# A decoder layer on one core: two norms' squares summed by GpSimd, the last norm applied by rows and stored in quarters

## The chip, the cores and the metric

The kernel runs on one core of a Trainium2 chip. The metric is the device time of one execution in microseconds (us), and the comparison is by the median of several executions. A core has TensorE (matmuls; PE in the profile, its weight loads PEld), VectorE (DVE), ScalarE (ACT), GpSimd (POOL) and SyncE (SP), each with its own instruction stream. They wait for each other by semaphores only, and 16 transfer engines move data on their behalf.

## The reference, cut to what matters

One step of a decoder layer on 256 prompt tokens and 8 sample tokens, 264 columns in all, with 2048 channels. The mixer in front of these lines (gated DeltaNet and a short convolution) is not touched.

```python
def rmsnorm(x, g):
    r = xf * lax.rsqrt(jnp.mean(xf * xf, axis=-1, keepdims=True) + EPS)
    return r * g
...
    h = h + mixed @ w_o
    hn = rmsnorm(h, ffn_norm)
    h = h + (jax.nn.silu(hn @ w_ffn_gate) * (hn @ w_ffn_up)) @ w_ffn_down
    hn = rmsnorm(h, ple_norm)
    h = h + jax.nn.sigmoid(hn @ w_ple_gate) * (p_i @ w_ple_proj)
...
    y_prompt = rmsnorm(hp, final_norm)
    y_sample = rmsnorm(hs, final_norm)
```

## The kernel before, in words

The activations lie transposed in SBUF: `h` has 16 tiles of 128 channels by 264 tokens. Every weight matrix is streamed once from memory, in *pieces* of 4 x 128 rows by 256 columns (512 KB; 3 or 2 x 128 rows in the down projections, 2 in the ple projection). SyncE loads a piece into one of four `raw` buffers (L447), ScalarE rounds it into `whi` (L951), VectorE subtracts to get `wlo` (L1238), and TensorE multiplies each 128-row slice and each of two 128-column tiles three times (L675): xhi by whi, xlo by whi, xhi by wlo, 24 matmuls a piece. Splits run three pieces ahead (`AHEAD`). Four pieces over all 2048 rows make a *pair* of output tiles in two PSUM banks, and pairs alternate between banks 0, 1 and banks 2, 3.

The order is written out by hand: a list of phases, each with its pairs, and every engine walks this list with its own code for each piece (`extra(ph, it, j)`, j the piece in the phase) and each pair (`evac`). At the end of the list stand `wo`, then `ffn0r`, `ffn0s`, `down0` and `ffn1r`, `ffn1s`, `down1` (the two halves of the ffn), `pproj` (the ple projection) and the ple gate, eight pairs in three phases, `pgate_first`, `pgate` and `pgate_last`. `wo`, `down0`, `down1` and `pgate` are loops with two pairs in the body.

A norm works so: ScalarE squares each of the 16 tiles of `h` into `sqh` (L961), TensorE multiplies each by a matrix of ones and adds them up in bank 4 (`norm_sums`), VectorE makes the mean and its reciprocal (L1270, L1272), ScalarE the root, and every pair is multiplied by `rstd` at its eviction (L1487). So the weights can be multiplied by the unnormed, gain-scaled `h` first. For the ffn and the ple norm four squares and four sums follow each of the phase's first four pieces. For the final norm two squares and two sums follow each of the first seven pieces of `pgate_last`, and the last two come behind the last pair. Then VectorE multiplies the 16 tiles by gain and `rstd` (L1646), TensorE turns them in blocks of 128 by 128 (L926), ScalarE copies them out of PSUM (L1224), and SyncE stores 128 rows at a time (L460) and then the 8 sample rows (L462).

A gate pair is evicted in three steps: VectorE multiplies by `rstd` (L1487), ScalarE takes the sigmoid (L1122), VectorE multiplies by the projection `pp` and adds to `h` (L1500, L1505).

Of the kernel before, what the change touches and what calls it, by code (L numbers as in the profile page):

```python
# [35 lines left out]
ds = bass.ds  # L36
# [54 lines left out]
def trunk(nc, I, O):  # L91
# [120 lines left out]
    sqh = at("sqh", [P, DTL, N], F32, regO)  # L212
# [12 lines left out]
    with ctx:  # L225
# [91 lines left out]
        def layer_pairs(gx):  # L317
# [12 lines left out]
            Phase("wo", 4, [mk(wo, lambda it, n=n: (2 * it + n) * COLS, X, "addh", (lambda it, n=n: 2 * it + n), xr="mix") for n in range(2)]),  # L330
# [5 lines left out]
        for half in range(2):  # L336
            for part, lo_, n_ in (("r", 0, FP - NB), ("s", FP - NB, NB)):
# [86 lines left out]
        NORM = {"first": 0, "ffn0r": 1, "pgate_first": 2}  # L424
        PREV = lambda ph: phases[phases.index(ph) - 1]

        def vcol(i):
            return vec[:, ds(i, 1)]
# [5 lines left out]
        def _(sp):  # L434
# [235 lines left out]
        def _(pe):  # L670
# [6 lines left out]
            def norm_sums(n, tiles=range(DTL)):  # L677
# [5 lines left out]
                if tiles[-1] == DTL - 1:  # L683
                    m.then_inc(sum_ready, 1)
# [991 lines left out]
```

## Time and profile before

| | |
|---|---|
| three runs | 2762.25, 2772.05, 2767.54 us; median 2767.54 us |
| the profiled execution | 2767.79 us; its span 2766.3 us, mean granted TensorE clock 0.982 |
| busy, share of the span | TensorE 96%, VectorE 60%, ScalarE 48%, GpSimd 16% |
| chain that ended last | TensorE 58%, transfers 2%, VectorE, GpSimd and ScalarE 1% each |
| moved | 505.25 MB, mean 183 GB/s |

The chain is followed back from the last instruction, at each step to what released it. Where it names TensorE's matmul line, nothing held TensorE. Times in the rows are us from the start of the span, unless a column says ns. A row `[0.87 <-ACT sqh L961]` means that the engine stood idle for 0.87 us before it, until that line of that engine had finished. An fp32 matmul with the ones stands as two instructions in the trace, so `x8` there are four sums.

### The profile page before, as it was taken

How to read it: one execution, taken by the hardware profiler on the slowest of the kernel's cores; microseconds unless marked ns; L12 is line 12 of the kernel's file. 1: busy time of each engine (PE TensorE's matmuls, PEld its weight loads, DVE VectorE, ACT ScalarE, POOL GpSimd, SP SyncE). 2: the span in 40 equal slices, each digit the busy share in tenths (PEclk: the TensorE clock that was granted, in tenths of full speed). 3: DMA queues.
4: the chain of work that ended last, by engine and by line, in shares of the span. 5: the costliest groups of instructions: out<-in, count | busy, mean ns of one | idle time of the engine just before them, and what ended most of it. 6: DMA issues, size and time to landing. Idle time of an engine off the chain costs nothing.

```text
span 2766.3 us, 54613 instructions
## 1 busy us (share of the span) xinstructions
PE 2641.9 (96%) x21133; PEld 2597.2 (94%) x21133; DVE 1653.7 (60%) x2851; ACT 1325.2 (48%) x2010; POOL 453.6 (16%) x845
## 2 busy tenths in 40 slices
PE   6999999999999999999999999999999999999997
PEld 4999999999999999999999999999999999999997
DVE  4757576666757475633354555456676656776664
ACT  5526454453535353443443344344665545655553
POOL 1425160515243341000000000000110000100000
PEclk9999999999999999999999999999999999999998
DMA  5545464545545555767655555746997567985542
GB/s 167 163 136 159 133 173 116 173 136 154 143 141 141 154 144 146 207 190 214 201 171 183 167 167 166 252 141 194 304 319 248 181 195 233 320 275 185 172 159 82
DMA packets 441663, 505.25 MB, mean 183 GB/s; under 512 B 19521, under 2 KB 421690, under 8 KB 438658
## 3 DMA queue, kind: packets, MB, share of 16 engines
q1 hardware_dynamic: 415264, 415.42, 49.2%
q0 software_dynamic: 25664, 87.47, 10.1%
q8 instruction: 107, 1.75, 0.3%
q14 instruction: 50, 0.41, 0.0%
q10 hardware_dynamic: 578, 0.19, 0.0%
HBM read 477.10 MB, written 26.49 MB: 182 GB/s over the span
## 4 chain that ended last, share of the span: by engine, by line
PE 58%; DMA 2%; DVE 1%; POOL 1%; ACT 1%; issue 1%; DVEq 0%; ACTq 0%; SPq 0%; POOLq 0%
PE bank L675 57%; DMA raw<-in_w_o 1%; POOL sol L546 1%; POOL prod L543 0%; ACT xhi L965 0%; DMA raw<-in_w_ffn_down 0%; DVE xlo L1266 0%; DVE wlo L1238 0%; ACT whi L951 0%; DMA blk<-blk_scratch 0%; DVE h L1646 0%; PE bank L926 0%; DMA raw<-in_w_ple_gate 0%; DMA DT<-sol_scratch 0%; DMA sol_scratch<-sol 0%
## 5 line engine op out<-in xcount | busy, mean ns | idle before, releaser
L675 PE MATMUL bank<-xhi,whi 128*128 128x264 f32 x5520 | 1602.7, 290 | 36.9 <-DVE wlo L1238 16.5
L675 PE MATMUL bank<-xlo,whi 128*128 128x264 f32 x5520 | 1573.9, 285 | 0.0
L675 PE MATMUL bank<-xhi,wlo 128*128 128x264 f32 x5520 | 1571.3, 285 | 0.0
L1238 DVE TENSOR_TENSOR wlo<-raw,whi 128x1024 fp32r<-128x1024 f32 x828 | 1009.9, 1230 | 824.5 <-ACT whi L951 823.0
L951 ACT ACTIVATE whi<-raw 128x1024 fp32r<-128x1024 f32 x828 | 870.9, 1057 | 854.2 <-PE bank L675 763.1
L675 PEld LDWEIGHTS bank<-xhi,whi 128*128 128x128 f32 x5520 | 1047.0, 190 | 44.3 <-issue 37.1
L675 PEld LDWEIGHTS bank<-xlo,whi 128*128 128x128 f32 x5520 | 1047.5, 190 | 2.6 <-issue 1.9
L675 PEld LDWEIGHTS bank<-xhi,wlo 128*128 128x128 f32 x5520 | 1044.6, 189 | 0.0
L675 PE MATMUL bank<-ahi,whi 128*128 128x264 f32 x704 | 200.7, 285 | 2.0 <-DVE wlo L1238 2.0
L675 PE MATMUL bank<-ahi,wlo 128*128 128x264 f32 x704 | 200.8, 285 | 0.0
L675 PE MATMUL bank<-alo,whi 128*128 128x264 f32 x704 | 200.4, 285 | 0.0
L675 PEld LDWEIGHTS bank<-ahi,whi 128*128 128x128 f32 x704 | 133.1, 189 | 2.2 <-DVE wlo L1238 2.2
L675 PEld LDWEIGHTS bank<-ahi,wlo 128*128 128x128 f32 x704 | 133.3, 189 | 0.0
L675 PEld LDWEIGHTS bank<-alo,whi 128*128 128x128 f32 x704 | 133.0, 189 | 0.0
L546 POOL TENSOR_TENSOR sol<-sol,prod 128x60 f32<-128x60 f32 (+24 forms) x248 | 123.8, 499 | 19.5
L648 POOL DMA_DIRECT2D out_gdn_s<-sS x16 | 18.7, 1171 | 607.6 <-DVE sS L1603 607.6
L543 POOL TENSOR_TENSOR prod<-blk,sol 128x60 f32<-128x60 f32 (+24 forms) x248 | 114.7, 462 | 19.5
L1383 DVE SCALAR_TENSOR_TENSOR cacc<-cin,vec,cacc 128x288 f32<-128x288 f32 x224 | 108.4, 525 | 4.0
L1157 ACT ACTIVATE sS<-sS,bc 128x128 f32<-128x128 f32 x256 | 81.2, 392 | 0.0
L1603 DVE SCALAR_TENSOR_TENSOR sS<-sD,kqs,sS 128x128 f32<-128x128 f32 x256 | 72.6, 346 | 0.0
L520 POOL DMA_DIRECT2D st_qkv<-in_state_qkv_conv x32 | 16.8, 528 | 292.0 <-PE bank L675 292.0
L675 PEld LDWEIGHTS bank<-kqs,chunkS 128*128 128x128 f32 x512 | 62.8, 191 | 0.0
(280 smaller groups left out, 1846.2 us busy)
## 6 DMA issues: line engine op xcount, KB each, us to landing
raw<-in_w_in SPq DMA_DIRECT2D x356, 512.0 KB, 3.9
raw<-in_w_ffn_gate SPq DMA_DIRECT2D x88, 512.0 KB, 5.5
raw<-in_w_ffn_up SPq DMA_DIRECT2D x88, 512.0 KB, 4.8
raw<-in_w_ffn_down SPq DMA_DIRECT2D x96, 384.0 KB, 2.9
raw<-in_w_gdn_out SPq DMA_DIRECT2D x64, 512.0 KB, 3.3
chunkS<-in_state_gdn POOLq DMA_DIRECT2D x16, 1024.0 KB, 7.4
raw<-in_w_sconv_out SPq DMA_DIRECT2D x32, 512.0 KB, 3.4
raw<-in_w_o SPq DMA_DIRECT2D x32, 512.0 KB, 3.3
```

What stands on the lines that cost most here:

```text
L520: pool.dma_start(st_qkv[:, i % 2, :, :], stq[:, ds(STATE_COL[i](grp), COLS)].rearrange("r (t p) -> r t p", p=P)).then_inc(st_in[i % 2], 16)
L543: mine.inc(pool.tensor_tensor(prod[:, 0:m, 0:n], blk[:, j, j + 1:SB].unsqueeze(1).to_broadcast([P, m, n]), sol[:, 0:m, j:j + 1].to_broadca ...
L546: mine.inc(pool.tensor_tensor(sol[:, 0:m, j + 1:SB], sol[:, 0:m, j + 1:SB], prod[:, 0:m, 0:n], ALU.add))
L648: pool.dma_start(O["gdn_s"][0, 2 * b2 + s, 16 * c:16 * c + 16, :, :].rearrange("h k v -> k h v"), sS[:, s, :, :]).then_inc(n_stored[s], 16)
L675: return pe.matmul(out, lhsT, rhs, start=start, stop=stop)
L951: act.activation(whi[:, at_ % SPLIT, :, :], raw[:, at_ % RAW, :, :], ACT.Copy).then_inc(hi_ready, 1)
L1157: m = act.activation(sS[:, s, i, :], sS[:, s, i, :], ACT.Copy, scale=bc[:, ds(it * 2 + (s + 1), 1), 16 * c + i:16 * c + i + 1].rearrange(" ...
L1238: dve.tensor_tensor(wlo[:, at_ % SPLIT, :, :], raw[:, at_ % RAW, :, :], f32(whi[:, at_ % SPLIT, :, :]), ALU.subtract).then_inc(lo_ready, 1)
L1383: m = dve.scalar_tensor_tensor(out=cacc[:, t, :], in0=x, scalar=w, in1=cacc[:, t, :], op0=ALU.mult, op1=ALU.add)
L1603: m = dve.scalar_tensor_tensor(out=sS[:, s, i, :], in0=sD[:, s, i, :], scalar=kqs[:, 8 * c + i // 2, ds(it * 2 + s, 1), 0], in1=sS[:, s, i ...
```

## The change

- `wo`, `down0`, `down1` and the ple gate become one written-out phase each, with eight pairs.
- In `wo` and `down1` ScalarE squares each finished pair of `h` in one instruction of 528 elements (`acc_square`), the first into `acc`, the others into `et`, behind the second split of the next pair; the eighth comes in the next phase's first piece. GpSimd adds them into `acc` (`squares_in`). TensorE sums over the partitions with two matmuls behind the third piece (`acc_sums`).
- In the gate phase TensorE turns a finished pair of `h` into banks 5, 6 and 7 (two prompt blocks and the 8 sample rows), behind piece 4i+6 (`turn_out`). ScalarE squares these with an accumulator into a column of `ssum` (`out_squares`), VectorE multiplies them by the final gain into `yrow` (`out_gains`). The gain stands along the row, so GpSimd loads a copy of it for each of the 128 partitions.
- Behind the last pair VectorE adds the eight columns of `ssum`, and mean, reciprocal and root work on three columns (`rs`). Then ScalarE scales block 0, VectorE block 1 and GpSimd the sample rows by `rs`. Blocks 0 and 1 are done and stored in quarters of 512 channels.

```diff
-            Phase("wo", 4, [mk(wo, lambda it, n=n: (2 * it + n) * COLS, X, "addh", (lambda it, n=n: 2 * it + n), xr="mix") for n in range(2)]),
+            Phase("wo", 1, [mk(wo, lambda it, n=n: n * COLS, X, "addh", const(n), xr="mix") for n in range(NPB)]),
...
-        phases.append(Phase("pgate_first", 1, [mk(wpg, lambda it, n=n: n * COLS, X, "pg", const(n), xr="ple") for n in range(2)]))
-        phases.append(Phase("pgate", NPB // 2 - 2, [mk(wpg, lambda it, n=n: (2 * it + n) * COLS, X, "pg", (lambda it, n=n: 2 * it + n), xr="ple") for n in (2, 3)]))
-        phases.append(Phase("pgate_last", 1, [mk(wpg, lambda it, n=n: n * COLS, X, "pg", const(n), xr="ple") for n in (NPB - 2, NPB - 1)]))
+        phases.append(Phase("pgate", 1, [mk(wpg, lambda it, n=n: n * COLS, X, "pg", const(n), xr="ple") for n in range(NPB)]))
...
+        def turned_at(ph, j, lag):
+            i = (j - lag) // 4
+            return i if ph.name == "pgate" and j >= lag and (j - lag) % 4 == 0 and i < NPB - 1 else None
...
-            for b in range(BLK):
-                sp.wait_ge(y_copied, DTL // 4 * (b + 1))
-                sp.dma_start(yo[0, b * P:(b + 1) * P, :], yrow[:, b, :]).then_inc(out_stored, 16)
-            sp.wait_ge(y_copied, DTL // 4 * (BLK + 1))
+            for q in range(4):
+                c = slice(512 * q, 512 * q + 512)
+                for b in range(BLK):
+                    sp.wait_ge(y_out[b], q + 1)
+                    sp.dma_start(yo[0, b * P:(b + 1) * P, c], yrow[:, b, c]).then_inc(out_stored, 16)
+            sp.wait_ge(y_out[BLK], 1)
             sp.dma_start(O["y_sample"][:, 0, :], yrow[0:NB, BLK, :]).then_inc(out_stored, 16)
...
+            def squares_in(n):
...
+                for i in range(1, NPB):
+                    pool.wait_ge(acc_sq, NPB * n + i + 1)
+                    pool.wait_ge(acc_done, (NPB - 1) * n + i - 1) if n or i > 1 else None
+                    pool.tensor_tensor(acc[:, :, :], acc[:, :, :], et[:, 2 * (i % 2):2 * (i % 2) + 2, :], ALU.add).then_inc(acc_done, 1)
...
+            squares_in(0)
...
+            pool.memset(ssum[:, :, :], 1.0).then_inc(ssum_set, 1)
+            squares_in(1)
+            pool.dma_start(gain[:, :], I["final_norm"].partition_broadcast(P)).then_inc(gain_in, 16)
+            pool.wait_ge(rstd_ready, 4)
+            pool.wait_ge(y_gained, NPB)
+            pool.tensor_tensor(yrow[0:NB, BLK, :], yrow[0:NB, BLK, :], rs[0:NB, BLK:BLK + 1].to_broadcast([NB, D]), ALU.mult).then_inc(y_out[BLK], 1)
...
+            def acc_sums(n):
+                pe.wait_ge(acc_done, (NPB - 1) * n)
+                mm(bank[4][:, 0:N], ones[:, :], acc[:, 0, :], True, False)
+                mm(bank[4][:, 0:N], ones[:, :], acc[:, 1, :], False, True).then_inc(sum_ready, 1)
+            def turn_out(i):
+                freed(pe, by["pgate"], 0, i)
+                if i > 0:
+                    pe.wait_ge(y_gained, i)
+                for b in range(BLK + 1):
+                    r = P if b < BLK else NB
+                    for t in range(2):
+                        c = P * t
+                        m = pe.transpose(bank[5 + b][0:r, c:c + P], h[:, 2 * i + t, b * P:b * P + r], ident[:, :])
+                m.then_inc(y_turned, 1)
...
-                elif ph.name in NORM and j < 4:
-                    norm_sums(NORM[ph.name], range(4 * j, 4 * j + 4))
-                elif ph.name == "pgate_last" and j < 7:
-                    norm_sums(3, range(2 * j, 2 * j + 2))
+                elif ph.name == "first" and j < 4:
+                    norm_sums(range(4 * j, 4 * j + 4))
+                elif ph.name in ("ffn0r", "pgate") and j == 2:
+                    acc_sums(NORM[ph.name])
+                elif turned_at(ph, j, 6) is not None:
+                    turn_out(turned_at(ph, j, 6))
...
-            norm_sums(3, range(DTL - 2, DTL))
-            n = 0
-            for b in range(BLK + 1):
-                r = P if b < BLK else NB
-                for k4 in range(DTL // 4):
-                    pe.wait_ge(y_ready, 4 * k4 + 4)
-                    if n >= 4:
-                        pe.wait_ge(y_copied, n - 3)
-                    for k in range(4):
-                        m = pe.transpose(bank[n % 4][0:r, k * P:(k + 1) * P], h[:, 4 * k4 + k, b * P:b * P + r], ident[:, :])
-                    m.then_inc(y_turned, 1)
-                    n += 1
+            turn_out(NPB - 1)
...
+            def acc_square(ph, i):
...
+                n = NORM["ffn0r" if ph.name == "wo" else "pgate"] - 1
+                freed(act, ph, 0, i)
+                if i > 2:
+                    act.wait_ge(acc_done, (NPB - 1) * n + i - 2)
+                dst = acc[:, :, :] if i == 0 else et[:, 2 * (i % 2):2 * (i % 2) + 2, :]
+                act.activation(dst, h[:, 2 * i:2 * i + 2, :], ACT.Square).then_inc(acc_sq, 1)
+            def out_squares(i):
+                act.wait_ge(y_turned, i + 1)
+                if i == 0:
+                    act.wait_ge(ssum_set, 1)
+                c = slice(COLS * (i % 2), COLS * (i % 2) + COLS)
+                for b in range(BLK + 1):
+                    r = P if b < BLK else NB
+                    act.activation(junk[0:r, b, c], bank[5 + b][0:r, 0:COLS], ACT.Square, accum_out=ssum[0:r, b, i:i + 1]).then_inc(y_squared, 1)
...
+                elif q.kind == "addh":
+                    if ph.name in SUMMED and qi < NPB - 1:
+                        acc_square(ph, qi)
...
-                    if j == 0:
-                        freed_all(act, by["pgate"])
-                    elif j == 6:
-                        freed(act, ph, it, 0)
-                    squares(h, sqh, range(2 * j, 2 * j + 2))
+                if turned_at(ph, j, 7) is not None:
+                    out_squares(turned_at(ph, j, 7))
+                elif ph.name in ("ffn0r", "pproj") and j == 0:
+                    acc_square(by["wo" if ph.name == "ffn0r" else "down1"], NPB - 1)
...
-                        if q.kind in ("qkv", "sh") and qi + 1 < len(ph.pairs):
+                        if q.kind in ("qkv", "sh", "addh") and qi + 1 < len(ph.pairs):
                             late = qi
...
-            freed_all(act, by["pgate_last"])
-            squares(h, sqh, range(DTL - 2, DTL))
+            act.activation(junk[:, 0, 0:1], eps[:, :], ACT.Sqrt)
+            out_squares(NPB - 1)
             act.wait_ge(mean_ready, 4)
-            act.activation(rstd[:, :], rstd[:, :], ACT.Sqrt).then_inc(rstd_ready, 1)
-            n = 0
-            for b in range(BLK + 1):
-                r = P if b < BLK else NB
-                for k4 in range(DTL // 4):
-                    act.wait_ge(y_turned, n + 1)
-                    act.activation(yrow[0:r, b, k4 * 512:(k4 + 1) * 512], bank[n % 4][0:r, :], ACT.Copy).then_inc(y_copied, 1)
-                    n += 1
+            act.activation(rs[:, :], rs[:, :], ACT.Sqrt).then_inc(rstd_ready, 1)
+            act.wait_ge(rstd_ready, 4)
+            act.wait_ge(y_gained, NPB)
+            for q in range(4):
+                c = slice(512 * q, 512 * q + 512)
+                act.activation(yrow[:, 0, c], yrow[:, 0, c], ACT.Copy, scale=rs[:, 0:1]).then_inc(y_out[0], 1)
...
+            def out_gains(i):
+                if i == 0:
+                    dve.wait_ge(gain_in, 16)
+                for b in range(BLK + 1):
+                    r = P if b < BLK else NB
+                    dve.wait_ge(y_squared, (BLK + 1) * i + b + 1)
+                    m = dve.tensor_tensor(yrow[0:r, b, COLS * i:COLS * i + COLS], bank[5 + b][0:r, 0:COLS], gain[0:r, COLS * i:COLS * i + COLS], ALU.mult)
+                m.then_inc(y_gained, 1)
...
+                elif turned_at(ph, j, 7) is not None:
+                    out_gains(turned_at(ph, j, 7))
...
             walk(dve, work, (mine,), dve_per)
-            norm_mean(3)
-            for kt in range(DTL):
-                dve.scalar_tensor_tensor(out=h[:, kt, :], in0=h[:, kt, :], scalar=vec[:, 352 + kt:353 + kt], in1=rstd[:, :],
-                                         op0=ALU.mult, op1=ALU.mult).then_inc(y_ready, 1)
+            out_gains(NPB - 1)
+            for n in (4, 2, 1):
+                mine.inc(dve.tensor_tensor(ssum[:, :, 0:n], ssum[:, :, 0:n], ssum[:, :, n:2 * n], ALU.add))
+                mine.settle(dve)
+            mine.inc(dve.tensor_scalar(rs[:, :], ssum[:, :, 0], 1.0 / D, EPS, ALU.mult, ALU.add))
+            mine.settle(dve)
+            dve.reciprocal(rs[:, :], rs[:, :]).then_inc(mean_ready, 1)
+            dve.wait_ge(rstd_ready, 4)
+            dve.wait_ge(y_gained, NPB)
+            for q in range(4):
+                c = slice(512 * q, 512 * q + 512)
+                dve.tensor_scalar(yrow[:, 1, c], yrow[:, 1, c], rs[:, 1:2], None, ALU.mult).then_inc(y_out[1], 1)
```

How the instructions stand, at the places that the prediction speaks of. `L` is the line in the kernel of that list.

TensorE in `ffn0r`, before: the end of the first piece, its four sums, and the start of the second piece; three more such blocks follow.

```order
L675 MATMUL bank<-xhi,whi 128x264
L675 MATMUL bank<-xlo,whi 128x264
L675 MATMUL bank<-xhi,wlo 128x264
L675 MATMUL bank<-sqh,ones 128x264 x4
L675 MATMUL bank<-xhi,whi 128x264
L675 MATMUL bank<-xlo,whi 128x264
L675 MATMUL bank<-xhi,wlo 128x264
```

And now: the end of the third piece, and the only block of sums.

```order
L699 MATMUL bank<-xhi,whi 128x264
L699 MATMUL bank<-xlo,whi 128x264
L699 MATMUL bank<-xhi,wlo 128x264
L699 MATMUL bank<-acc,ones 128x264 x2
L699 MATMUL bank<-xhi,whi 128x264
L699 MATMUL bank<-xlo,whi 128x264
L699 MATMUL bank<-xhi,wlo 128x264
```

Sixteen sums in four blocks became two in one, two pieces later. ScalarE now, around the end of `wo` and the start of `ffn0r` (before it had no square in `wo`, and after the 16 scaled tiles four blocks of `sqh<-h 128x264 x4`, each behind a split):

```order
L998 ACTIVATE et<-h 128x528
L983 ACTIVATE whi<-raw 128x1024 x4
L998 ACTIVATE et<-h 128x528
L983 ACTIVATE whi<-raw 128x1024 x2
L1012 ACTIVATE xhi<-h,vec 128x264 x16
L983 ACTIVATE whi<-raw 128x1024
L998 ACTIVATE et<-h 128x528
L983 ACTIVATE whi<-raw 128x1024 x3
L1188 ACTIVATE rstd<-rstd 128x264
```

The squares moved ahead, between the splits of `wo`, and the last of them stands where the first four stood. TensorE in the gate phase now, between two pieces:

```order
L699 MATMUL bank<-xlo,whi 128x264
L699 MATMUL bank<-xhi,wlo 128x264
L724 MATMUL bank<-ident,h 128x128 x4
L724 MATMUL bank<-ident,h 8x128 x2
L699 MATMUL bank<-xhi,whi 128x264
L699 MATMUL bank<-xlo,whi 128x264
```

Six transposes stand where `pgate_last` had two sums. VectorE's last rows now, where it had 16 multiplies of `h`:

```order
L1563 TENSOR_TENSOR h<-h,et 128x264 x2
L1330 TENSOR_TENSOR yrow<-bank,gain 128x256 x2
L1330 TENSOR_TENSOR yrow<-bank,gain 8x256
L1706 TENSOR_TENSOR ssum<-ssum 128x3x4
L1706 TENSOR_TENSOR ssum<-ssum 128x3x2
L1706 TENSOR_TENSOR ssum<-ssum 128x3
L1708 TENSOR_SCALAR rs<-ssum 128x3
L1710 RECIPROCAL rs<-rs 128x3
L1715 TENSOR_SCALAR yrow<-yrow,rs 128x512 x4
```

Gain, sum of the columns, mean and reciprocal are followed by four quarters of block 1. GpSimd's last rows now (the loads of `prow` were its last before):

```order
L684 DMA prow<-in_p_sample 8x256
L685 MEMSET ssum 128x24
L667 TENSOR_TENSOR acc<-acc,et 128x528 x7
L687 DMA gain<-in_final_norm 128x2048
L690 TENSOR_TENSOR yrow<-yrow,rs 8x2048
```

Its queue goes on behind them with the adds of `down1`, the gain and the sample rows.

## Rows read from the trace of the kernel before

**Rows 1.** The chain that ended last: start us, us, what
```profile
1107.26 316.53 PE bank L675 x2644
...
1833.03 0.42 ACT sqh L961
1833.49 264.69 PE bank L675 x2156
...
2621.67 4.30 DMA raw<-in_w_ple_gate
```

**Rows 2.** Timeline of TensorE, norms' first pieces: start us, us, engine, line
```profile
1833.49 2.05 PE L675 MATMUL bank<-sqh,ones 128*128 128x264 f32 x8 [0.87 <-ACT sqh L961]
...
1847.68 1.94 PE L675 MATMUL bank<-sqh,ones 128*128 128x264 f32 x8
...
2635.42 2.05 PE L675 MATMUL bank<-sqh,ones 128*128 128x264 f32 x8 [0.70 <-ACT sqh L961]
```

**Rows 3.** Timeline of TensorE, the last two gate pairs
```profile
2713.62 1.16 PE L675 MATMUL bank<-sqh,ones 128*128 128x264 f32 x4 [1.03 <-ACT sqh L961]
...
2736.55 1.05 PE L675 MATMUL bank<-sqh,ones 128*128 128x264 f32 x4
```

**Rows 4.** Groups by line and form, GpSimd: busy us, mean ns | idle us
```profile
L539 POOL COPY sol<-unit 128x256 f32<-128x256 f32 x8 | 4.1, 511 | 49.1 <-DMA blk<-blk_scratch 49.1
...
L546 POOL TENSOR_TENSOR sol<-sol,prod 128x70 f32<-128x70 f32 x8 | 2.5, 315 | 0.6
...
L546 POOL TENSOR_TENSOR sol<-sol,prod 128x50 f32<-128x50 f32 x8 | 2.2, 276 | 0.6
```

**Rows 5.** Timeline of ScalarE, before the ple projection
```profile
2611.66 1.06 ACT L951 ACTIVATE whi<-raw 128x1024 fp32r<-128x1024 f32 x1
```

**Rows 6.** Windows: us, busy of PE PEld DVE ACT POOL, PEclk, DMA share, GB/s
```profile
2614.00:2618.00 4.00, 4.00 (x24) 4.00 (x24) 1.22 (x1) 2.36 (x6) 0.00 (x0) 0.65 0.20 66
2622.00:2626.00 4.00, 3.95 (x33) 3.74 (x31) 3.44 (x3) 3.47 (x8) 0.00 (x0) 1.00 0.85 275
```

**Rows 7.** Timeline of TensorE, the end
```profile
2755.78 6.25 PE L926 MATMUL bank<-ident,h 128*128 128x128 f32 x36 [0.50 <-DVE h L1646]
```

**Rows 8.** Window at the end, columns as in rows 6
```profile
2750.00:2760.00 10.00, 7.56 (x32) 6.36 (x33) 5.73 (x15) 4.09 (x7) 0.00 (x0) 0.50 0.17 68
```

**Rows 9.** Timeline of VectorE, the end
```profile
2742.90 0.78 DVE L1505 TENSOR_TENSOR h<-h,et 128x264 f32<-128x264 f32 x2
...
2749.17 6.56 DVE L1646 SCALAR_TENSOR_TENSOR h<-h,vec,rstd 128x264 f32<-128x264 f32 x16 [0.49 <-ACT rstd L1218]
```

**Rows 10.** Groups by line and form, ScalarE
```profile
L994 ACT ACTIVATE Tt<-bank 128x128 f32<-128x128 f32 x32 | 8.1, 254 | 3.1 <-PE bank L675 3.1
...
L994 ACT ACTIVATION_READ_ACCUMULATOR Tt<-bank 128x1 f32 x32 | 6.0, 188 | 0.0
...
L1224 ACT ACTIVATE yrow<-bank 128x512 f32<-128x512 f32 x8 | 4.8, 598 | 7.0 <-PE bank L926 7.0
```

**Rows 11.** Groups by line and form, VectorE
```profile
L1339 DVE TENSOR_SCALAR Nn<-kTok,tokk 128x128 f32<-128x128 f32 x64 | 13.2, 280 | 0.0
...
L1405 DVE TENSOR_SCALAR prep<-prep 32x264 f32<-32x264 f32 x1 | 0.3, 345 | 0.0
```

**Rows 12.** Timeline of VectorE, start of ffn0r
```profile
1833.16 1.23 DVE L1238 TENSOR_TENSOR wlo<-raw,whi 128x1024 fp32r<-128x1024 f32 x1 [0.45 <-ACT whi L951]
```

**Rows 13.** Timelines of VectorE and GpSimd, 383 to 388 us
```profile
383.51 3.83 DVE L1238 TENSOR_TENSOR wlo<-raw,whi 128x1024 fp32r<-128x1024 f32 x3
...
386.35 1.18 POOL L543 TENSOR_TENSOR prod<-blk,sol 128x75 f32<-128x75 f32 x1
387.61 0.35 POOL L546 TENSOR_TENSOR sol<-sol,prod 128x75 f32<-128x75 f32 x1
```

**Rows 14.** Timeline of SyncE, the end
```profile
2762.85 0.31 SPq L462 DMA_DIRECT2D out_y_sample<-yrow  x1
```

**Rows 15.** Transfers in 40 slices of 2756 to 2767 us
```profile
GB/s 0 0 0 60 0 0 0 0 209 417 328 477 477 477 447 357 357 268 0 0 0 477 477 477 447 387 328 357 387 477 239 0 0 0 0 0 0 0 0 0
```

More of the change, by code:

```diff
@@ L211, in trunk @@
     assert 8 * HALF * N + 16 * N <= 4 * (HV + DTL) * N
-    sqh = at("sqh", [P, DTL, N], F32, regO)
+    acc = at("acc", [P, 2, N], F32, regS + 17408)
+    ssum = at("ssum", [P, BLK + 1, NPB], F32, regS + 17408 + 2112)
+    rs = at("rs", [P, BLK + 1], F32, regS + 17408 + 2112 + 128)
+    junk = at("junk", [P, BLK + 1, 2 * COLS], F32, regS + 17408 + 2112 + 256)
+    assert regS + 17408 + 2112 + 256 + 8 * COLS * (BLK + 1) <= end
+    gain = at("gain", [P, D], F32, regO)
     prow = at("prow", [P, BLK + 1, PD], F32, regS)
@@ L423, in trunk @@
                     "first": {8: ("exponents",), 9: ("lt",)}}
[L424 to L428, printed above, removed]
+        NORM = {"first": 0, "ffn0r": 1, "pgate": 2}
+        SUMMED = ("wo", "down1")
+        def turned_at(ph, j, lag):
+            i = (j - lag) // 4
+            return i if ph.name == "pgate" and j >= lag and (j - lag) % 4 == 0 and i < NPB - 1 else None
         block = ctx.enter_context(nc.Block())
@@ L675, in mm, with norm_sums @@
                 return pe.matmul(out, lhsT, rhs, start=start, stop=stop)
-            def norm_sums(n, tiles=range(DTL)):
+            def norm_sums(tiles):
                 for kt in tiles:
-                    pe.wait_ge(sq_ready, DTL * n + kt + 1)
-                    src = sqr if n == 0 else sqh
-                    m = mm(bank[4][:, 0:N], ones[:, :], src[:, kt, :], kt == 0, kt == DTL - 1)
+                    pe.wait_ge(sq_ready, kt + 1)
+                    m = mm(bank[4][:, 0:N], ones[:, :], sqr[:, kt, :], kt == 0, kt == DTL - 1)
                 if tiles[-1] == DTL - 1:
                     m.then_inc(sum_ready, 1)
+            def acc_sums(n):
[12 more added lines that the diff above has]
+                m.then_inc(y_turned, 1)
             def gdn(slot, gr):
@@ L957, in split_ahead @@
                 split(it * (ph.pieces // RAW * 16) + 16 * (at_ // RAW + 1), at_, it * ph.pieces + at_ + 1)
-            def squares(src, dst, tiles):
-                for kt in tiles:
-                    act.activation(dst[:, kt, :], src[:, kt, :], ACT.Square).then_inc(sq_ready, 1)
+            def acc_square(ph, i):
[13 more added lines that the diff above has]
+                    act.activation(junk[0:r, b, c], bank[5 + b][0:r, 0:COLS], ACT.Square, accum_out=ssum[0:r, b, i:i + 1]).then_inc(y_squared, 1)
             def scaled_hi(gain):
@@ L1127, in extra @@
                     gdn(step, gr)
-                if ph.name == "pgate_last" and j < 7:
-                    if j == 0:
-                        freed_all(act, by["pgate"])
-                    elif j == 6:
-                        freed(act, ph, it, 0)
-                    squares(h, sqh, range(2 * j, 2 * j + 2))
+                if turned_at(ph, j, 7) is not None:
+                    out_squares(turned_at(ph, j, 7))
+                elif ph.name in ("ffn0r", "pproj") and j == 0:
+                    acc_square(by["wo" if ph.name == "ffn0r" else "down1"], NPB - 1)
                 elif ph.name in NORM and j < 4:
-                    squares(*((hpro, sqr) if ph.name == "first" else (h, sqh)), range(4 * j, 4 * j + 4))
+                    if ph.name == "first":
+                        for kt in range(4 * j, 4 * j + 4):
+                            act.activation(sqr[:, kt, :], hpro[:, kt, :], ACT.Square).then_inc(sq_ready, 1)
                     if j == 3:
```

19 lines of the change are left out of this document (11 added, 8 removed).

## Prediction

> **What bounds the kernel now.** I read the chain that ended last first. Through the body it is TensorE at its own pace: 316.53 us for 2644 matmuls in the written-out groups (0.120 us each), 264.69 us for 2156 from 1833.49 on (0.123, with one norm's sums among them) [rows 1]. There only less work on TensorE, or a wait before it that goes, shortens the run. After the last gate matmul (2740.5) the chain goes through every engine in turn, and there each handover counts. So I price four places: the ffn norm, the ple norm, the eight gate pairs, the end.
>
> **The two norms whose squares go to GpSimd.** Before, each of the first four pieces (24 matmuls) is followed by 4 sums. From the first block of sums to the fourth is 14.19 us, 4.73 a period [rows 2]; in the last gate pairs, with 2 sums a piece, six periods take 22.93 us, 3.82 each [rows 3]. The difference gives 0.455 us a sum and leaves 2.91 us a piece. 14 of 16 sums go: 14 x 0.455 = 6.4 us. TensorE also stood 0.87 us (ffn) and 0.70 us (ple) for the first squares [rows 2]. With the sums behind the third piece that wait goes, if the running sum is there. ScalarE makes the last square where its first one stood, at 1833.03 [rows 1], so it is there at about 1833.7; the third piece ends about 1838.4 (1833.49 - 0.87 + two pieces). GpSimd has 4.7 us for one add. No row has an add of 128x528; one of 128x50 takes 276 ns and one of 128x70 315 ns [rows 4]: 1.95 ns an element, 0.18 + 1.03 = 1.2 us. Bounds: nothing, or an add held by a VectorE split before it starts (1.23 us), together 2.4 us, still under 4.7. I take no cost. The seven adds before it have a pair of pieces each, 11.6 us, and ScalarE's seven squares in a phase lie behind a split, of which three are always ahead of TensorE. Gain: 7.3 us (ffn) and 7.1 us (ple).
>
> **The gain row.** GpSimd issues a new 1 MB transfer behind its last add. ScalarE squares the last down pair behind the split that begins at 2611.66 [rows 5]; with 0.6 us for the square and 1.2 for the add that is about 2614.5. The transfer engines carry little then (share 0.20 in 2614 to 2618) but 0.85 in 2622 to 2626 [rows 6], and the chain waits 4.30 us for w_ple_gate at 2621.67 [rows 1]. Bounds: nothing, and all of it, 3.8 us at that stretch's 275 GB/s. Most should fit in the quiet part; I take 1.0 us lost.
>
> **The gate pairs.** Out go 14 sums, 6.4 us, and a wait of 1.03 us [rows 3]. In come 7 x 6 transposes. At the end of before 36 of them take 6.25 us [rows 7] at a granted clock of 0.50 [rows 8], 1.04 us for six; at the full clock that would be 0.52. So seven sets cost 3.6 to 7.3 us; among full-clock matmuls, with a handover each, I take 5.0. Squares and gain multiplies (under 2 us a pair on engines that have 11.6) are hidden: pair i is turned after piece 4i+6, three pieces behind its last matmul, when its h is written. Gain 2.4 us. Writing the loops out costs nothing: loop and written-out stretches run alike [rows 1].
>
> **The end**, in the clock of before. The last h is there at 2742.90 + 0.78 = 2743.7 [rows 9].
> - Handover 0.2, six transposes at the low clock 1.3 with the last one's length: 2745.2.
> - Three squares with accumulator. A 128-wide one is 254 ns, a 512-wide eviction 598, so 256 wide is about 0.37, and a read of the accumulator 188 [rows 10], partly overlapped: 0.45 each, 2746.6. The last gain multiply 0.4: 2747.0.
> - Five operations on 3 columns, each behind the one before, at 0.2: 2748.0. Root: 2748.4. In before the first scaled h came at 2749.17, and 16 of them took 6.56 us more [rows 9]; transposes and evictions followed those.
> - Scaling. ScalarE's first quarter is there at 2749.0, then one each 0.5 us. VectorE: tensor_scalar took 280 ns for 128 columns and 345 for 264 [rows 11], 0.48 ns a column, against 1.2 in the two-input split (1.23 us for 1024 [rows 12]). 512 columns: 0.46 us. GpSimd: 8 rows, but 2048 elements in each: 0.18 + 2048 x 1.95 ns = 4.2 us.
>
> Here is the one new wait that matters. While VectorE ran three splits back to back (383.51 to 387.34), GpSimd's 75-element multiply took 1.18 us, and its next instruction of that size 0.35; VectorE took 3.83 us for the three instead of 3 x 1.23 [rows 13]. The two take a port in turns, an instruction at a time. I take it that the fast tensor_scalar needs what the splits need (no row shows it). So GpSimd's multiply slips in behind VectorE's first quarter (2748.9) and holds the other three until 2753.1. SyncE issues in order, block 0 then block 1 of each quarter: the fourth store waits until 2753.6, four more stand behind it at 0.4 each, and y_sample goes out at 2755.6. Before, y_sample's issue to the end was 2766.3 - 2762.85 = 3.45 us [rows 14], which gives 2759.1; the five late quarters of 256 KB, at about 400 GB/s [rows 15] 0.65 us each, run from 2754.4 to 2757.7 and end with 1.8 us of completion at 2759.5. The later one counts: the end gains 6.8 us.
>
> The Trainium skill, "SBUF — State Buffer", Who interferes with whom, has it as a rule: VectorE in a 2-port mode, or with two SBUF inputs, and GpSimd take the shared port pair as an exclusive lock for a whole instruction. By it VectorE stands for all of GpSimd's multiply; the trace agrees for short ones (1.18 against 0.35 us), and no row has a long one. The Trainium skill, "GPSIMD Engine Reference", 3.1 Elementwise, gives 4497 ns for a tensor_tensor add of 2048 fp32 elements; with it the end would be 0.3 us later than in my sum.
>
> **Sum.** 7.3 + 7.1 - 1.0 + 2.4 + 6.8 = 22.6 us. The profiled execution took 2767.8 us (the median of the three runs is 2767.5), so 2745.2, say **2745 us**. Its own range: gate transposes -1.4 or +2.3; the gain row +1.0 or -2.8; GpSimd's price per element 1.3 ns at the least, as in its 256-element copy (511 ns) [rows 4], 1.3 us earlier, and 4.5 ns at the most, if 315 ns for 70 had no fixed part, 5 us later. As they seldom fall together: 2742.5 to 2748.5.
>
> **Rivals.**
> 1. *No hold at the end.* VectorE's quarters all pass before GpSimd. The stores then run from 2750.0 at 0.65 us each to 2755.2, the end is 2757.2: 9.1 us instead of 6.8; with the gain row free 2742. For it: the four multiplies stand back to back, and both engines leave from one semaphore. Against: GpSimd got in between splits each time [rows 13]. 0.20.
> 2. *Transfer and port take more.* The gain row costs 3.8 us, and the last multiply holds 2 us longer: 2748.5 to 2751. For it the share of 0.85 [rows 6], against it the issue at about 2614.5. 0.15.
> 3. *The sums were not TensorE's bound.* ScalarE and VectorE come late out of the 16 tiles they scale and split. With the sums gone TensorE could wait for the fourth split, and half of each norm's gain is lost: 2752. Against: that split ends at 1834.4 [rows 12] and the fourth piece begins about 1839.3. 0.08.
> 4. *Slower.* Four phases written out add some 2300 matmuls to the program. If the supply of instructions slowed TensorE there (wo, down and gates are some 440 us, 3640 matmuls), 0.127 instead of 0.121 us each would eat the 22.6 us, and from 0.1295 us on (31 us lost, 2776) the kernel is slower. Against: the written-out groups run at 0.120 [rows 1]. 0.02.
>
> **How the numbers follow.** Main case 0.52, rival 1 0.20, rival 2 0.15, rival 3 0.08, rival 4 0.02, better than all 0.03. The range 2740.5 to 2751 leaves out rivals 3 and 4 and the better case, under 2 in 10. Within 0.3% (8.3 us, about what this measurement can tell from no change) needs two thirds of the sum to fail. Faster 0.95, same 0.03, slower 0.02.
>
> **What would show it in the profile after.** Two sums, not sixteen, in each norm, and no TensorE wait before them. A period of 11.6 + 0.7 us per gate pair. The wait for w_ple_gate about 5.3 instead of 4.3 us. GpSimd's last multiply 4.2 us long, VectorE's second quarter only behind it. From the last gate matmul to the end 19.0 instead of 25.8 us. The prediction falls if TensorE waits for the running sum, if the first turned pair waits for the gain row, or if matmuls in the written-out phases take over 0.123 us.

## The result and the profile after

| | before | after |
|---|---|---|
| median of five runs | 2762.25 us | 2743.13 us (2734.73 to 2748.06) |
| ratio, 95% interval | | 0.9919 (0.9901 to 0.9937) |
| profiled execution, its span | 2767.79, 2766.3 us | 2741.38, 2739.9 us |

The kernel became faster by 0.8%, or 22.4 us by the ratio; the forecast was 22.6 us. The two medians lie 19.1 us apart, the two profiled executions 26.4 us. The interval of the ratio runs from 17.4 to 27.3 us, so the agreement to 0.2 us is luck. The median of 2743.1 us lies in the range of 2740.5 to 2751. But that range was stated for a kernel before of 2767.5 us; set on the 2762.25 us measured beside it, the ratio gives 2739.9 us, 0.6 us under its lower end. Most of the way from the 2745 us forecast to there is the kernel before, whose five executions lie between 2760.4 and 2772.1 us. The term that was sized too small is the end: 6.8 us forecast, 8.4 measured.

The engine row of the page after: busy us, share of the span, instructions.

```profile
PE 2613.8 (95%) x21045; PEld 2574.7 (94%) x21045; DVE 1660.3 (61%) x2866; ACT 1323.2 (48%) x2019; POOL 482.5 (18%) x862
```

The chain that ended last, of the kernel after: start us, us, what.

```profile
1822.38 3.28 issue
1825.66 243.97 PE bank L699 x1996
...
2608.87 6.29 DMA raw<-in_w_ple_gate
...
2618.58 3.65 issue
2622.23 22.91 PE bank L699 x172
2645.14 0.66 PE bank L724 x6
2645.79 11.63 PE bank L699 x96
2657.43 0.66 PE bank L724 x6
...
2718.89 0.66 PE bank L724 x6
...
2722.51 0.79 DVE bank L1545 x2
...
2725.68 0.89 PE bank L724 x6
2726.59 0.48 ACT junk L1008 x2
2727.09 1.12 DVE yrow L1330 x3
...
2729.13 0.21 ACT rs L1268
2729.37 0.49 DVE yrow L1715
2729.85 3.74 DVEq L230
2733.59 0.79 DVE yrow L1715 x2
```

Read it against [rows 1]. At `ffn0r` one stretch of TensorE runs from its first matmul at 1825.66 on, and the square that stood in the chain at 1833.03 is gone. The gate pairs are all alike: 0.66 us of transposes and 11.63 of matmuls, where [rows 3] had 3.82 us a piece with two sums and a wait. From the last gate matmul (2722.47) to the end are 17.4 us, before 25.8. One thing in it is new and long: 3.74 us at 2729.85, in which VectorE has issued its second quarter and doesn't get to run it.

Next the one block of sums, in timelines of VectorE, GpSimd and TensorE: start, us, instruction. Before, four blocks with a wait ahead of the first stood here [rows 2].

```profile
1830.89 1.23 DVE L1286 TENSOR_TENSOR wlo<-raw,whi 128x1024 fp32r<-128x1024 f32 x1 [0.45 <-ACT whi L983]
1832.37 3.33 DVE L1286 TENSOR_TENSOR wlo<-raw,whi 128x1024 fp32r<-128x1024 f32 x2 [0.26 <-ACT whi L983]
...
1831.47 1.83 POOL L667 TENSOR_TENSOR acc<-acc,et 128x528 f32<-128x528 f32 x1 [14.22 <-ACT et L998]
...
1836.02 1.05 PE L699 MATMUL bank<-acc,ones 128*128 128x264 f32 x4
```

The last add ends at 1833.30, the third piece at 1836.02: no idle time stands at the sums' row, so the running sum was there 2.7 us early. The add shows 1.83 us, not the 1.2 that I had worked out, but it began in a split of VectorE that ended at 1832.12: from there to its end are 1.18 us. VectorE's next two splits took 3.33 us for 2 x 1.23, 0.8 us held in their turn. The groups by line and form have the same for all 14 adds, each of which begins 0.58 us into a split, and the mean of a transpose:

```profile
L667 POOL TENSOR_TENSOR acc<-acc,et 128x528 f32<-128x528 f32 x14 | 25.7, 1833 | 203.9 <-ACT et L998 203.9
...
L724 PE MATMUL bank<-ident,h 128*128 128x128 f32 x32 | 4.8, 274 | 3.2 <-DVE h L1563 3.2
```

And the end, in timelines of VectorE, GpSimd and SyncE:

```profile
2729.37 5.02 DVE L1715 TENSOR_SCALAR yrow<-yrow,rs 128x512 f32<-128x512 f32 x4 [0.27 <-ACT rs L1268]
...
2729.42 3.88 POOL L690 TENSOR_TENSOR yrow<-yrow,rs 8x2048 f32<-8x2048 f32 x1 [122.54 <-ACT rs L1268]
...
2730.11 5.91 SPq L470 DMA_DIRECT2D out_y_prompt<-yrow  x8
2736.07 0.60 SPq L472 DMA_DIRECT2D out_y_sample<-yrow  x1
```

VectorE's four quarters take 5.02 us in place of 4 x 0.49. GpSimd's multiply starts at 2729.42, in the first quarter, and ends at 2733.30; the second quarter ends 0.3 us later, at 2733.59.

**Where the 26.4 us of the two traces lie.** I cut both at the first matmul of `ffn0r`, of the ple projection's transposes and of the gate phase, and behind the last gate matmul:

| stretch | before | after | gain | forecast |
|---|---|---|---|---|
| up to `ffn0r` | 1827.9 | 1825.7 | 2.3 | 0 |
| first four pieces of `ffn0r` with sums | 21.33 | 14.18 | 7.15 | 7.3 |
| from there to the projection | 760.8 | 761.4 | -0.6 | 0 |
| ple projection | 20.0 | 21.0 | -1.0 | -1.0 |
| first four gate pieces | 21.17 | 14.04 | 7.1 | 7.1 |
| the rest of the gate phase | 89.3 | 86.2 | 3.1 | 2.4 |
| last gate matmul to the end | 25.8 | 17.4 | 8.4 | 6.8 |

The first and third rows are code that the change leaves alone, or the load waits of `wo` and `down0`, and they differ from run to run: in all traces of this study `ffn0r` begins between 1821.0 and 1838.3 us. So traces are compared from `ffn0r` on: 938.4 us before, 914.2 after.

### The profile page after: what moved, and what is told of

It is laid out like the page before. It is cut to its first block, busy times and chain, and to the rows that moved or that the text cites. A ratio compares the mean times of both kernels' runs of the same rounds, so it can differ in the third digit from the quotient of the medians.

```text
span 2739.9 us, 53487 instructions
## 1 busy us (share of the span) xinstructions
PE 2613.8 (95%) x21045; PEld 2574.7 (94%) x21045; DVE 1660.3 (61%) x2866; ACT 1323.2 (48%) x2019; POOL 482.5 (18%) x862
## 4 chain that ended last, share of the span: by engine, by line
PE 58%; DMA 3%; POOL 1%; issue 1%; DVE 1%; ACT 0%; DVEq 0%; ACTq 0%; POOLq 0%
PE bank L699 57%; DMA raw<-in_w_ffn_down 1%; DMA raw<-in_w_o 1%; POOL prod L553 1%; POOL sol L556 0%; DVE wlo L1286 0%; DMA blk<-blk_scratch 0%; ACT whi L983 0%; DMA raw<-in_w_ple_gate 0%; PE bank L724 0%; DMA sol_scratch<-sol 0%; DMA DT<-sol_scratch 0%; DVEq L230 0%; DVE xlo L1314 0%; DMA blk_scratch<-Tt 0%
## 5 line engine op out<-in xcount | busy, mean ns | idle before, releaser
L553 POOL TENSOR_TENSOR prod<-blk,sol 128x60 f32<-128x60 f32 (+24 forms) x248 | 125.9, 508 | 19.5
L556 POOL TENSOR_TENSOR sol<-sol,prod 128x60 f32<-128x60 f32 (+24 forms) x248 | 111.9, 451 | 19.4
L632 POOL DMA_DIRECT2D chunkS<-in_state_gdn x16 | 18.5, 1154 | 265.9 <-PE bank L699 139.4
```

The costliest lines, as they stand in the source:

```text
L553: mine.inc(pool.tensor_tensor(prod[:, 0:m, 0:n], blk[:, j, j + 1:SB].unsqueeze(1).to_broadcast([P, m, n]), sol[:, 0:m, j:j + 1].to_broadca ...
L556: mine.inc(pool.tensor_tensor(sol[:, 0:m, j + 1:SB], sol[:, 0:m, j + 1:SB], prod[:, 0:m, 0:n], ALU.add))
L632: pool.dma_start(chunkS[:, c, :, :], I["state_gdn"][0, b, 16 * c:16 * c + 16, :, :].rearrange("h k v -> k h v")).then_inc(s_in[c], 16)
```

## The experiments

Times of each against the kernel before on the same chip, and the stretches of its one trace. "To the end" is counted from `ffn0r`'s first matmul, "tail" from the last gate matmul's end, and "turn" is the last six transposes, which lie in the tail.

| kernel | median us | ratio (95%) | projection | turn | tail | to the end |
|---|---|---|---|---|---|---|
| before | | | 20.0 | | 25.8 | 938.4 |
| changed | 2743.1 | 0.9919 (0.9901-0.9937) | 21.0 | 0.87 | 17.4 | 914.2 |
| e7, changed again | 2743.1 | 0.9902 (0.9877-0.9928) | 19.9 | 1.24 | 17.75 | 913.5 |
| e1_sample_dve | 2731.7 | 0.9864 (0.9835-0.9893) | 20.8 | 1.54 | 16.65 | 913.2 |
| e2_pool_last | 2737.6 | 0.9898 (0.9859-0.9937) | 20.7 | 0.87 | 16.0 | 910.2 |
| e3_gain_late | 2741.8 | 0.9904 (0.9871-0.9938) | 20.6 | 1.54 | 18.05 | 912.1 |
| e4_final_only | 2753.8 | 0.9947 (0.9927-0.9967) | 20.7 | 0.88 | 17.4 | 928.4 |
| e5_sums_first | 2750.6 | 0.9940 (0.9922-0.9958) | 21.7 | 1.54 | 18.05 | 920.5 |
| e6_whole_stores | 2750.1 | 0.9935 (0.9912-0.9957) | 20.1 | 1.27 | 17.7 | 912.9 |
| e8_best | 2744.8 | 0.9909 (0.9881-0.9937) | 20.0 | 1.33 | 16.45 | 911.2 |
| e9_warm | 2740.1 | 0.9900 (0.9879-0.9922) | 19.8 | 0.88 | 16.0 | 909.0 |
| e10_warm_more | 2734.5 | 0.9874 (0.9849-0.9900) | 20.1 | 0.87 | 16.0 | 907.0 |

The intervals reach 5 to 11 us to either side, so a step of 1 to 2 us is read from the stretches, not from the medians.

### e1: the sample rows on VectorE

```diff
-            pool.wait_ge(rstd_ready, 4)
-            pool.wait_ge(y_gained, NPB)
-            pool.tensor_tensor(yrow[0:NB, BLK, :], ...).then_inc(y_out[BLK], 1)
...
+            dve.tensor_scalar(yrow[0:NB, BLK, :], yrow[0:NB, BLK, :], rs[0:NB, BLK:BLK + 1], None, ALU.mult).then_inc(y_out[BLK], 1)
```

> VectorE scales the 8 sample rows behind its four quarters; GpSimd does nothing at the end. Theory (GpSimd's 3.88 us multiply holds VectorE's second quarter from 2729.85 to 2733.6): VectorE's quarters take 0.49 us each without a gap, the sample rows about 1.1 us (0.48 ns for each of 2048 columns), and the stores run on without the hole between 2731.5 and 2734; from the last gate matmul to the end about 15.7 us instead of 17.4. Rival (VectorE's second quarter is slow by itself, or for ScalarE's sake): it stays at 3.8 us, and the end at 17.4 or, with the sample rows behind it, 18.5.

Timelines of VectorE and SyncE in e1:

```profile
2728.64 1.68 DVE L1712 TENSOR_SCALAR yrow<-yrow,rs 128x512 f32<-128x512 f32 x4 [0.27 <-ACT rs L1265]
2730.23 1.27 DVE L1713 TENSOR_SCALAR yrow<-yrow,rs 8x2048 f32<-8x2048 f32 x1
...
2729.39 4.49 SPq L470 DMA_DIRECT2D out_y_prompt<-yrow  x8
```

Four quarters in 1.68 us, without a gap, and nothing late in SyncE's eight issues (4.49 instead of 5.91 us). The second quarter is not slow by itself, nor for ScalarE's sake, which works beside it as before. The tail is 16.65 us and not 15.7, because the transposes took 1.54 us here; without them it is 15.1 us, against 16.5 in the changed kernel.

### e2: GpSimd's multiply behind VectorE's quarters

```diff
             pool.wait_ge(y_gained, NPB)
+            pool.wait_ge(y_out[1], 4)
             pool.tensor_tensor(yrow[0:NB, BLK, :], ...)
```

> GpSimd keeps the sample rows but waits until VectorE's fourth quarter is done. Theory (the hold is one instruction of GpSimd against VectorE): the four quarters back to back in 2.0 us, GpSimd's multiply then from about 2731.4 to 2735.2 on the changed kernel's clock, the sample store issued at once, the end 3.6 us later: about 16.5 us behind the last gate matmul. The multiply's length tells whether it was itself prolonged: 3.8 to 3.9 us again if it was alone before. Rival (no hold between these two): second quarter still long, and the end at 19 us or later.

Timelines of VectorE and GpSimd in e2:

```profile
2724.56 1.67 DVE L1716 TENSOR_SCALAR yrow<-yrow,rs 128x512 f32<-128x512 f32 x4 [0.27 <-ACT rs L1269]
...
2726.41 3.59 POOL L691 TENSOR_TENSOR yrow<-yrow,rs 8x2048 f32<-8x2048 f32 x1 [123.96 <-DVE yrow L1716]
```

Again 1.67 us for the four. The multiply alone takes 3.59 us, and 3.88 when it met VectorE's first quarter. The same work, only later, and the tail is 16.0 us, 1.4 us shorter (16.5 was expected). So it is the meeting of these two instructions that costs, and the rival falls. The Trainium skill, "GPSIMD Engine Reference", 3.1 Elementwise, has 4497 ns for a tensor_tensor add of 2048 fp32 elements; this multiply, with one operand repeated along the row, took 3590.

### e3: the gain row late

```diff
             squares_in(1)
+            pool.wait_ge(sum_ready, 3)
             pool.dma_start(gain[:, :], ...)
```

> GpSimd issues the gain transfer only when TensorE has made the ple norm's sums (about 2633), 27 us later than now. Theory (this 1 MB takes the place of w_ple_gate's first pieces): the wait for w_ple_gate in the chain goes from 6.3 to about 4.3 us, the ple projection is 1.0 us shorter, and no wait appears before the first turned pair, as 7.6 us of transfer end at about 2641 and the pair is turned at 2645. Rival (the longer projection has another cause, the square and the add put in there): it stays at 21.0 us.

The chain of waits of e3 over the projection:

```profile
2605.85 13.42 PE bank L700 x96
2619.27 4.55 issue
```

No wait for `w_ple_gate` is left in this chain (e4 and e8, with the transfer late too, still have 4.9 us of it in theirs), and the 96 matmuls pass in 13.42 us; but the wait ahead of the gate phase is 4.55 us, 3.65 before this edit, and the projection with its transposes took 20.6 us. The mechanism shows best in the pairs: in all six traces with the early transfer the eighth pair begins 2.0 to 3.3 us behind the seventh, in all five with the late one, and before, 1.45 us. What reaches the gate phase is less. The six early ones took 19.9 to 21.7 us, mean 20.7, the five late ones 19.8 to 20.7, mean 20.2: a difference of about 0.5 us, half of the 1.0 us that the first pair of traces shows and that was expected here. Even this is not cleanly the transfer's. In six of these eleven traces, and in the one of before, some 15 of the stretch's first matmuls ran at the lower clock. Where they ran at the full one, the means are 20.0 us early (e6, e7) and 20.0 late (e8, e9, e10); where they ran at the lower one, 21.0 early (the first trace, e1, e2, e5) and 20.6 late (e3, e4), while the kernel before, with no such transfer, took 20.0. So the term was in the right place and at least twice too large, and what is left of it is not told apart from the spread.

### e4: the final norm alone

```diff
-                elif ph.name == "first" and j < 4:
-                    norm_sums(range(4 * j, 4 * j + 4))
-                elif ph.name in ("ffn0r", "pgate") and j == 2:
-                    acc_sums(NORM[ph.name])
+                elif ph.name in NORM and j < 4:
+                    norm_sums(NORM[ph.name], range(4 * j, 4 * j + 4))
```

With it the 16 squares as before, no `acc_square`, no adds, and the late gain row.

> The final norm by rows and quarters as in the changed kernel, with the gain transfer late; the ffn and the ple norm with 16 squares and 16 sums each as in the kernel before. Theory (sums are TensorE's own time): each norm costs 7.3 us more than in the changed kernel, with TensorE waits of 0.9 and 0.7 us for the first square, so 14.6 minus 1.0 us slower than it, about 0.45% faster than the kernel before (10.2 less 7.3, and 8.4, is 11.3 us). Rival (the written-out loops or the freed engines gave part of the gain): the norms cost other than 7.3 us, and the ratio to the kernel before moves off 0.9955 by more than 0.002.

TensorE at the ffn norm in e4:

```profile
1831.73 2.05 PE L699 MATMUL bank<-sqh,ones 128*128 128x264 f32 x8 [0.89 <-ACT sqh L985]
```

The wait of 0.89 us and the sums are back, and four pieces take 21.35 us (ffn) and 21.17 us (ple), to a tenth what they took before, with `wo` and `down1` written out. From `ffn0r` on it is 14.2 us longer than the changed kernel, where 13.6 was expected; the ratio came at 0.9947 for 0.9955. The norms' gain is the sums', and the written-out loops neither give nor take.

### e5: the sums behind the first piece

```diff
-                elif ph.name in ("ffn0r", "pgate") and j == 2:
+                elif ph.name in ("ffn0r", "pgate") and j == 0:
```

> TensorE's two sums of each norm stand behind the first piece, not the third. Theory (the gain rests on the running sum being there in time, and the third piece is what covers it): the last add ends 7.65 us after TensorE's first matmul of ffn0r (1833.30 less 1825.65), the first piece 2.9 us, or 4.5 with slow matmuls, so TensorE waits 3.1 to 4.7 us in ffn0r. In the gate phase the adds were done 15 us before, so nothing there. Rival (splits or the scaled tiles hold TensorE in these pieces anyway): a wait that is made good by the fifth piece, and no loss in the stretch of four pieces.

TensorE in `ffn0r` in e5:

```profile
1828.67 2.13 PE L699 MATMUL bank<-acc,ones 128*128 128x264 f32 x4 [2.98 <-POOL acc L667]
```

It waits 2.98 us for the last add, just under the 3.1 to 4.7 expected, and the sums themselves take 2.13 instead of 1.05 us, at the lower clock. Four pieces took 18.92 us against 14.18: nothing is made good later (920.5 us from `ffn0r` on, against 914.2). The two pieces of cover are what makes the running sum free.

### e6: stores of whole blocks

```diff
-            for q in range(4):
-                for b in range(BLK):
-                    sp.wait_ge(y_out[b], q + 1)
-                    sp.dma_start(yo[0, b * P:(b + 1) * P, c], yrow[:, b, c]).then_inc(out_stored, 16)
+            for b in range(BLK):
+                sp.wait_ge(y_out[b], 4)
+                sp.dma_start(yo[0, b * P:(b + 1) * P, :], yrow[:, b, :]).then_inc(out_stored, 16)
```

> The final norm as in the changed kernel, but block 0, block 1 and the sample rows each stored whole, behind their last quarter. Theory (the quarters let the transfers begin 0.7 us after the root and overlap the hold): block 0 (1 MB) goes out at about 2732, block 1 at 2734.4, which end by rate (385 GB/s) at 2737.4 or later, so the end is 0 to 1 us later than now (17.4 to 18.5 us behind the last gate matmul). Rival (the quarters made the gain of the end): 3 us later.

SyncE at the end of e6:

```profile
2735.10 2.82 SPq L468 DMA_DIRECT2D out_y_prompt<-yrow  x2
2737.97 0.36 SPq L470 DMA_DIRECT2D out_y_sample<-yrow  x1
```

Without the transposes the tail is 16.45 us, with quarters 16.5. In this kernel the quarters gave nothing. That the hole which the hold makes in the stores eats what they gain by starting early is argued, not shown: no run stores whole blocks without the hold.

### e8, e9 and e10: both edits, and no idle TensorE

e8 joins e1 and e3. e9 and e10 add matmuls whose result nobody reads, at the places where TensorE else waits:

```diff
+            def warm(n):
+                for _ in range(n):
+                    mm(bank[4][:, 0:N], ones[:, :], vec[:, 0:N])
...
+                if ph.name in ("ffn0r", "pgate"):
+                    warm(7)
...
                     m.then_inc(p_turned, 1)
+                    warm(3)
             walk(pe, work)
+            warm(6)
             turn_out(NPB - 1)
```

> The late gain transfer and the sample rows on VectorE together. By the single ones: the end 16.0 us behind the last gate matmul where the last transposes run at the full clock, 16.7 at the half one, and a ple projection 0.3 us shorter; 1.7 us off the changed kernel, about 0.9913 of the kernel before. Rival: they share their cover and only the end's part is left.

> As the one before, and TensorE multiplies ones by a constant, into the unused bank 4, where it else stands idle: 7 matmuls ahead of ffn0r and of the gate phase, 3 ahead of the ple projection, 6 ahead of the last transposes. Theory (an idle stretch of 1.7 to 4 us brings the granted clock to its lower level, and some 15 matmuls behind it take 0.22 us instead of 0.12): no matmul with 0.22 us behind these four places; ffn0r's and the gate phase's first pieces 1.5 and 1.3 us shorter, the last six transposes 0.87 us; 3 us in all, about 0.9900. Rival (the slow matmuls come from something that the seams do, not from idleness): they stay, and 7 matmuls that end late cost up to 0.5 us a place.

The reason for the second: windows of the changed kernel just behind two waits of TensorE (us, busy time and instructions of PE, PEld, DVE, ACT and POOL, granted clock, DMA share, GB/s).

```profile
1826.50:1829.50 3.00, 3.00 (x17) 3.00 (x16) 3.00 (x8) 3.00 (x9) 0.00 (x0) 0.52 0.00 0
2622.60:2625.00 2.40, 2.40 (x12) 2.40 (x12) 2.40 (x7) 2.40 (x8) 0.00 (x0) 0.50 0.82 273
```

TensorE is busy all of the 3 us behind the wait ahead of `ffn0r`, but with 17 matmuls, at a granted clock of 0.52, the lower of its two levels, 1.2 GHz. Such a matmul takes 0.22 us and not 0.12, and 12 to 26 of them follow most of TensorE's waits of 1.5 us or more ahead of `ffn0r`, the projection and the gate phase, in the kernel before too.

e8's tail is 15.1 us without the transposes, as forecast. The projection took 20.0 us. Its first gate pieces ran at the lower clock (some 25 matmuls of 0.22 us), and from `ffn0r` on it took 911.2 us, 2.3 to 3.0 less than the changed kernel's two traces.

In e9 the slow matmuls are gone behind three of the four places: `ffn0r`'s four pieces took 12.60 us instead of 14.18, the last transposes 0.88, and the projection has none. One trace would not show that this is the idle matmuls' doing: `ffn0r` and the projection each had no slow matmuls in three of the ten traces without them, and the last transposes took 0.9 us in three of nine. But in e9 and in e10 all three places ran at the full clock. The gate phase did not in e9. Its chain, and a window:

```profile
2628.70 2.27 issue
2630.98 23.04 PE bank L697 x172
...
2631.00:2634.00 3.00, 3.00 (x15) 3.00 (x16) 3.00 (x8) 3.00 (x8) 0.00 (x0) 0.53 0.50 164
```

Behind the seven idle matmuls TensorE still stood 2.27 us, and ran at 0.53 then. That made e10 with 11 there.

> The changed kernel once more, beside the next one on the same chip, for its ratio and for a second trace. From ffn0r's first matmul to the end it should take 914 us again, within 1.5 us, and before ffn0r anything between 1823 and 1838 us, as in the traces so far: if the spread of the runs lies there, the change's own gain is 24 us in that part. Rival (the spread lies in the changed part): that part differs by over 3 us.

> As e9_warm, with 11 idle matmuls ahead of the gate phase in place of 7 (5.0 us, where TensorE still stood 2.66 us behind the seven and 15 matmuls at 0.22 us followed). Theory: no idle stretch over 1 us there and no slow matmuls, gate phase 1.5 us shorter from its first matmul to its last (98.9 instead of 100.4 us), its start at most 0.5 us later; from ffn0r's first matmul to the end about 907.5 us. Rival (any seam slows the clock): 100.4 us again.

The filling matmuls ahead of `ffn0r`, the chain at the gate phase and two windows of e10:

```profile
1821.32 3.28 PE L697 MATMUL bank<-vec,ones 128*128 128x264 f32 x14
...
2616.23 0.75 issue
2616.98 21.49 PE bank L697 x172
...
1826.00:1829.00 3.00, 3.00 (x27) 3.00 (x26) 3.00 (x8) 3.00 (x9) 0.00 (x0) 1.00 0.00 0
2617.20:2620.20 3.00, 3.00 (x26) 3.00 (x26) 3.00 (x9) 3.00 (x9) 0.00 (x0) 1.00 0.48 152
```

Seven matmuls (14 instructions) fill 3.28 us, the wait left is 0.17 us, and the first pieces run at 1.00. At the gate phase too: 98.8 us from its first to its last matmul, where e9 took 100.4. From `ffn0r` on 907.0 us, expected 907.5. e7 took 913.5 us there, 0.7 less than the first trace. So e10 is 6.4 us faster than the changed kernel in the part that both share, and 4.2 us faster than e8, from which it differs by the idle matmuls alone; on the chip that both ran on, the medians are 2734.5 and 2743.1 us.

The Trainium skill, "TensorE: Matmul & The Clock Gate", HAM oscillation — how this bites in real kernels, has it that TensorE's clock goes down while it waits and that the next work starts slow. The traces agree that work behind a wait can start slow, but the fall comes later: in the changed kernel the granted clock is 1.00 all through the wait ahead of `ffn0r` and still in 1825.7 to 1826.6, and only then the lower one. And it isn't certain: the wait of 3.3 us there (3.4 in the kernel before) was the same in all kernels without idle matmuls, and slow matmuls followed it in the kernel before, in the changed one, e1, e4, e5, e6 and e8, but not in e2, e3 and e7.

## Where the prediction was right, and where it was off

The mechanisms held, but the closeness of the sum, 22.6 against 22.4 us, is in part luck: in the part that the change touches, from `ffn0r` on, the two traces gained 24.2 us, and e7's 24.9. The step that failed is the size of the end, at 6.8 us, where 8.4 were measured. Step by step:

- *The norms.* 7.3 and 7.1 us forecast, 7.15 and 7.1 measured; e4 gives them back. (Where `ffn0r` began at the full clock, as in e7, its four pieces took 12.6 us.) The wait before the first sum went, as said. The add has 1.18 us of its own, 1.2 forecast, and 0.65 us in which it is held by the split that it meets, inside the bound of 2.4 us. The cover had 2.7 us left, and e5 shows what it is worth.
- *The gain row.* 1.0 us forecast, at most about 0.5 measured over eleven traces.
- *The gate pairs.* 2.4 us forecast. Six transposes with their handover took 12.29 - 11.63 = 0.66 us, 4.6 for the seven, not 5.0: I had stayed away from the full-clock end of my bounds, near which they ran, with 0.14 us of handover on 0.52. That makes 2.8; the stretch gained 3.1.
- *The end* is the step that was off: 8.4 us, not 6.8. Its mechanism held: GpSimd's multiply slips in behind VectorE's first quarter and holds the rest, and only the fourth store waits for it. Two sizes didn't. From the last `h` (2725.6) to the root took 3.7 us, not 4.7: handover and transposes took 0.9 us where I had 1.5 from the low clock, squares and last gains 1.65 for 1.8, the five small operations and the root 1.1 for 1.4. And GpSimd's multiply ended 4.0 us behind the root, not 4.7: it took 3.88, not 4.2 us, and started in the first quarter and not behind it. From its end to the end of the run are 6.6 us, forecast 6.4. The low clock alone doesn't make the difference: in e3 and e5, where the transposes took 1.54 us, the tail is 18.05 us and still 0.9 us shorter than the 19.0 forecast. The price of the hold was overrated as well: rival 1 had it at 2.3 us (by its own terms 2.5, as 2755.2 and 1.8 are 2757.0), and over eleven traces the tail without its transposes is 16.5 us with the hold and 15.1 without, 1.4 us.
- *Rival 1*, no hold, is what e1 and e2 made, not what happened. *Rival 2* fell with both of its sizes. *Rival 3*: TensorE had no wait at the fourth piece, and e4's loss is the whole gain. *Rival 4* fell: 96 matmuls of a gate pair, now written out, took 11.63 us, 0.121 each, and the stretch with both down projections 761.4 us for 760.8.
- What I had not counted is that the clock matters at the seams. The slow matmuls stood in the kernel before as well, so that in the first pair of traces they nearly cancel; but they cost 1.6 us at `ffn0r` alone and come in some executions only.

Left open: whether the gain row's transfer costs anything that the spread doesn't hide; why the lower clock follows one wait and not the same wait in the next execution. And the spread of 17 us up to `ffn0r`, which no experiment here touched.

## What to carry to other kernels

Sums that TensorE makes for a norm are worth their full time when TensorE is the bound; add the squares elsewhere first, and put the sum where two pieces of work cover the last add. An operation given to GpSimd "on the side" isn't free beside a critical VectorE: give the small one to VectorE, or put it last. And fill short waits of TensorE ahead of a long stretch of matmuls: behind idle stretches of 1.5 to 5.6 us the next 12 to 26 here mostly ran at half the clock.

## What the runs showed of the hardware

- Work in step on both engines meets each time: all 14 adds of GpSimd began 0.58 us into a VectorE split and took 1.83 us, of which 0.65 in its shadow; the split behind, where one was due, took 1.3 to 2.0 us instead of 1.23. GpSimd's multiply of 8 x 2048 took 3.59 us alone, 1.8 ns an element.
- VectorE's tensor_scalar of 128 x 512 took 0.49 us; one that met GpSimd's multiply 3.82 us. The hold is not only for two-input instructions.
- Idle stretches of 1.5 to 5.6 us ahead of `ffn0r`, the projection and the gate phase were mostly, and not always, followed by 12 to 26 matmuls at the lower clock. With 7 idle matmuls in 3.3 us ahead of `ffn0r`, and 11 ahead of the gate phase, none were.
